# Stick-breaking attention with two heads in a step, and LRU input parts queued behind the gates

## The chip, the cores and the metric

The kernel runs on one core of a Trainium2 chip. The metric is the device time of one execution in microseconds (us). TensorE (PE) multiplies matrices into PSUM, VectorE (DVE), ScalarE (ACT) and GpSimd (POOL) work elementwise, SyncE (SP) only issues DMAs here. Each engine takes its instructions strictly in the order of its own list and waits on semaphores for the others; PEld rows are TensorE's weight loads.

## The reference, cut to what matters

Two blocks are computed for 1024 positions of width 1024: a first block of two layers (window attention and memory attention, then an LRU mixer and memory attention, each with an MLP) and a second block with stick-breaking attention (8 heads) and sliding-window attention (8 heads). The change touches the LRU mixer and the stick-breaking attention:

```
# stick breaking, per head: q, k, v of 64 columns
z = q @ k.T * 0.125
log_1mb = where(causal, log_sigmoid(-z), 0.0)
later = reverse cumsum over keys of log_1mb, without the own term
w = where(causal, exp(log_sigmoid(z) + later), 0.0)
y = w @ v

# LRU, per direction (forward and reverse), per block of 128 channels
r = sigmoid(x @ wa + ba); i = sigmoid(x @ wx + bx)
log_a = -8 * r * softplus(-lam); a = exp(log_a)
u = sqrt(-expm1(2 * log_a)) * (i * x)
h[t] = a[t] * h[t-1] + u[t]
```

x of the LRU is a 4-tap convolution of a projection; the sum of both directions is multiplied by the gelu of a second projection.

## The kernel before, in words

Activations are kept transposed (channels on partitions, positions along the row). Every large product is written as three f32r matmuls of high and low parts (`project`). Weights arrive in blocks of 128x1024: `load` brings a block into one of NR buffers `raw` (4 before), `split` makes its high part on ACT and its low part on DVE (on POOL for the LRU layer's blocks) into `wsp`, two blocks ahead of TensorE, and a buffer of `raw` is loaded again as soon as its block is split. The program writes every engine's list by hand, in the order of the Python code; `Queues.add` adds an instruction with its waits.

**LRU.** For each of 8 channel blocks n: `lru_g(n)` evacuates the gelu projection, `lru_x(n+1)` the input projection of the next block and its convolution (one ACT instruction, then three DVE `STT`), `gates(n)` has four groups of six matmuls (`xs`, the split input parts, times `lruw`) with a Tanh each, then per direction Tanh, Exp, Square on ACT and the `v` product on DVE, then the gelu's Tanh, two Sqrt, the products `u` and the two scans (L1040). POOL adds the directions (L1042) and `L["late"]` multiplies by the gelu on DVE. `lru_parts(n+1)` makes the high part of the next block's input on ACT and the low part on DVE; before, it is called behind `gates(n)`, so its two instructions stand behind the square roots and the scans.

**Stick breaking.** A step is one head (par) of a pair (pr), a half of the queries (hf, 512 columns) and a key block kb of 128, from the last key block to the first; there are 96. On the diagonal a step covers only 128, 256 or 384 columns, so that of the 12 key blocks of a pair 6 are of full width and 2 each of 384, 256 and 128. A step does: scores z on TensorE; on DVE min(z/8, 40) from PSUM; on ACT Exp and Ln(1+.), which is softplus; on DVE max with z/8 (`STT`), on POOL its high part (CAST, L1253), on DVE its low part; on TensorE two matmuls with a triangle (`triI`) that add the sum within the block onto z in PSUM, and two with all ones (`onesN`) that add the block's whole sum to a running bank `AB` of the head; ACT copies z out of PSUM into `tw`, DVE adds the running bank, ACT takes Exp, and TensorE multiplies with v, whose columns are padded with 64 zeros so that both heads add into one bank. The parts of a step lie up to five steps apart on the engines' lists, with four score banks and three buffers of each kind.

Of the kernel before, what the change touches and what calls it, by code (L numbers as in the profile page):

```python
# [113 lines left out]
def program(nc, D, out, stop=None, dbg=None):  # L114
    ctx = ExitStack()
    with ctx:
# [34 lines left out]
        NR, NS, LA = 4, 3, 2  # L151
# [538 lines left out]
        def window_units(Qt, Kt, Vt, pairs, tiles, nbs, outf, bias, sinkv):  # L690
            units = []
            for n in range(8):
                for kp in range(pairs):
                    kbs = [n + d for d in nbs if 0 <= n + d < 8]
                    for half in range(2):
# [13 lines left out]
                        def pv(pts, ob, fr, n=n, kp=kp, kbs=kbs, half=half):  # L709
                            for j, (pt, c) in enumerate(pts):  # L710
                                for par in range(2):
                                    st = Vt[:, kbs[j], kp, 128 * par:128 * par + 64]
# [99 lines left out]
        Vt = place(48 * KB, [128, 8, 2, 192])  # L812
        MQ = place(64 * KB, [128, 4, 1024])
        pool(lambda e: e.memset(Vt[:, :, :, 64:128], 0.0), *kv_done)
# [37 lines left out]
        def rows_to(Tv, by_rms, *after):  # L852

            def ev(views, op):
                ends = []
                for t, v in enumerate(views):
                    C = v.shape[1] // 128
                    src = v.rearrange("p (c a d) -> p c a d", c=C, a=2)
                    dst = Tv[:, t, :, :].rearrange("p c (a d) -> p c a d", a=3)[:, :, 0:3:2, :]
# [142 lines left out]
        def gates(n):  # L1002

            gp = []
            for gi in range(4):
# [9 lines left out]
                if gi % 2 == 0:  # L1015
                    a = A(trs[d], ps, ACT.Tanh, op, L.get(("v", d)), L["r"], lam_ready, scale=0.5, bias=V("ba", i1))
                    L["tr"] = a
# [11 lines left out]
            L[("xc", n)] = [L[("o1", 1)], L["xs"], L["xsh"]]  # L1029
            a = A(gq, gq, ACT.Tanh, L["gq"], scale=0.7978845608028654)  # L1030
# [17 lines left out]
        for n in range(8):  # L1048
# [6 lines left out]
            if n < 7:  # L1055
                lru_parts(n + 1)
# [94 lines left out]
        SV = place(64 * KB, [128, 8, 4, 192])  # L1151
# [3 lines left out]
        pool(lambda e: e.memset(SV[:, :, :, 64:128], 0.0), *sv_free)  # L1155
# [21 lines left out]
        me = [place(o_ * KB, [128, 512]) for o_ in (28, 30, 94)]  # L1177
        sps = place(16 * KB, [128, 3, 2, 512], F32R)
        tw = place(88 * KB, [128, 3, 512])
        triI, onesN = triR[:, 0, :], triR[:, 1, :]  # L1180
        ZB, AB, OBK = (0, 1, 2, 3), (4, 5), (6, 7)
        steps = []
        grp = 0
        for pr in range(4):
            for hf in range(2):
                top = 4 * hf + 3
                for kb in range(top, -1, -1):
                    for par in range(2):
                        steps.append((pr, hf, kb, par, top, grp))
                grp += 1  # L1190
        n_s = len(steps)
        F = [dict() for _ in range(n_s)]
        got = lambda s, key: F[s].get(key) if s >= 0 else None

        def view(s):
            pr, hf, kb, par, top, grp = steps[s]
            c0 = max(0, kb - 4 * hf) * 128
            return (c0, PS[:, ZB[s % 4], c0:512], me[s % 3][:, c0:512], sps[:, s % 3, 0, c0:512],
                    sps[:, s % 3, 1, c0:512], tw[:, s % 3, c0:512], PS[:, AB[par], c0:512])

        def pe_scores(s):
            pr, hf, kb, par, top, grp = steps[s]
            c0, z = view(s)[:2]
            rows = slice(64 * par, 64 * par + 64)
            if kb == top and par == 0:
                ob = OBK[grp % 2]
                mm(PS[:, ob, :], zerob, cb[:, 0:512], True, False, c_cb, free[ob], skip_group_check=True)
            o = mm(z, SK[rows, pr, kb * 128:(kb + 1) * 128], SQ[rows, pr, 512 * hf + c0:512 * hf + 512], True, False,
                   free[ZB[s % 4]], skip_group_check=True)
            if kb >= 4 * hf:  # L1210
                o = mm(z[:, 0:128], identb, maskD, False, False, c_cb, skip_group_check=True)
            F[s]["qk"] = o

        def pe_cum(s):
            c0, z, m, sh, sl, t, ab = view(s)
            pr, hf, kb, par, top, grp = steps[s]
            if kb == top:
                F[s]["zero"] = mm(PS[:, AB[par], :], zerob, cb[:, 0:512], True, False, c_cb, free[AB[par]],
                                  skip_group_check=True)
            mm(z, triI, sh, False, False, F[s]["sh"], skip_group_check=True)  # L1220
            F[s]["cum"] = mm(z, triI, sl, False, True, F[s]["sl"], skip_group_check=True)

        def pe_carry(s):
            c0, z, m, sh, sl, t, ab = view(s)
            if steps[s][2] > 0:
                mm(ab, onesN, sh, False, False, F[s]["add"], skip_group_check=True)
                F[s]["carry"] = mm(ab, onesN, sl, False, False, skip_group_check=True)
            else:
                free[AB[steps[s][3]]] = [F[s]["add"]]
                F[s]["carry"] = None  # L1230

        def pe_values(s):
            pr, hf, kb, par, top, grp = steps[s]
            c0, z, m, sh, sl, t, ab = view(s)
            ob = OBK[grp % 2]
            o = mm(PS[:, ob, c0:512], SV[:, kb, pr, 64 * par:64 * par + 128], t, False, False, F[s]["w"],
                   skip_group_check=True)
            F[s]["pv"] = o
            if kb == 0 and par == 1:
# [3 lines left out]
        for s in range(n_s + 6):  # L1243
            v = s - 5
            if 0 <= v < n_s:
                pe_values(v)
            if s < n_s:
                pe_scores(s)
            v = s - 2
            if 0 <= v < n_s:  # L1250
                c0, z, m, sh, sl, t, ab = view(v)
                o = STT(m, z, 0.125, m, ALU.mult, ALU.max, F[v]["ln"])
                F[v]["sh"] = pool(lambda e, sh=sh, m=m: e.tensor_copy(sh, m), o, got(v - 3, "carry"),  # L1253
                                  got(v - 3, "cum"))
            v = s - 3
            if 0 <= v < n_s:
                c0, z, m, sh, sl, t, ab = view(v)
                F[v]["sl"] = TT(sl, m, fz(sh), ALU.subtract, F[v]["sh"], got(v - 3, "carry"), got(v - 3, "cum"))
                pe_cum(v)
            v = s - 4  # L1260
            if 0 <= v < n_s:
                c0, z, m, sh, sl, t, ab = view(v)
                F[v]["add"] = TT(t, t, ab, ALU.add, F[v]["zc"], got(v - 2, "carry"), F[v].get("zero"))
                pe_carry(v)
            if s < n_s:
                c0, z, m, sh, sl, t, ab = view(s)
                F[s]["min"] = TS(m, z, 0.125, 40.0, ALU.mult, ALU.min, F[s]["qk"], got(s - 3, "sl"), got(s - 3, "sh"))
            v = s - 1
            if 0 <= v < n_s:
                c0, z, m, sh, sl, t, ab = view(v)  # L1270
# [213 lines left out]
```

How the kernel before makes its waits and increments, by code:

```python
            def run(eng):  # L93
                seen = {}
                for o in self.q[name]:
                    for d in o.deps:
                        if seen.get(d.sem.name, 0) < d.val:
                            eng.wait_ge(d.sem, d.val)
                            seen[d.sem.name] = d.val
                    if o.fn is None:
                        continue
                    ins = o.fn(eng)
                    if o.sem is not None:
                        ins.then_inc(o.sem, 1 if o.sem is self.sems.get(name) else 16)
```

## Time and profile before

| | us |
|---|---|
| median of 2 runs | 3499.54 (3499.21 to 3499.87) |
| the profiled execution | 3512.42 |
| its span in the trace | 3510.6 |
| PE busy | 3225.2 (92%) |
| DVE busy | 1690.7 (48%) |
| ACT busy | 1084.7 (31%) |
| POOL busy | 392.4 (11%) |

The span is from the first to the last recorded instruction; the profiled execution's own time is 1.8 us more. Busy shares are averages over stages that have different limits, so a stage is read by itself: the LRU loop lies at 1474 to 1740 us of the span, stick breaking at 2913 to 3163 us.

### The profile page before, as it was taken

The page shows a single profiled execution, that of the slowest core. Times are in us where ns is not written, and L with a number is a line of the kernel's source. Part 1 is how long each engine was busy: PE and PEld are TensorE (multiplying, and loading weights), DVE is VectorE, ACT ScalarE, POOL GpSimd, SP SyncE. Part 2 cuts the span into 40 slices and gives each one's busy share as a digit, 9 for nine tenths or more (in the row PEclk, how much of TensorE's full clock was granted, in tenths as well). Part 3 has the DMA queues.
Part 4 walks back from the last instruction along what each step waited for, and adds up shares of the span by engine and source line. Part 5 has one row for each costly group of instructions (what it writes and reads, how often), then busy time and mean ns, then how long its engine had stood idle before and what let it go on. Part 6 is the DMA issues. An engine that isn't in the chain of part 4 may idle for free.

```text
span 3510.6 us, 35191 instructions
## 1 busy us (share of the span) xinstructions
PE 3225.2 (92%) x14288; PEld 2467.7 (70%) x14298; DVE 1690.7 (48%) x2178; ACT 1084.7 (31%) x1845; POOL 392.4 (11%) x313
## 2 busy tenths in 40 slices
PE   4999988999999999989879999999997999999768
PEld 4776546778888888767648788888885775548546
DVE  6544863254444433688642433333335416881355
ACT  4202652121111111466541211111114316771332
POOL 0001531000000000244310000000003102230120
PEclk9999999999999999999999999999998998999899
DMA  4210002122222211211211111111111310001012
GB/s 165 84 36 31 1 1 77 43 67 72 72 72 72 72 45 54 66 42 33 66 60 42 42 48 48 48 48 44 47 48 54 114 48 7 1 1 54 19 65 91
DMA packets 52578, 184.96 MB, mean 53 GB/s; under 512 B 5825, under 2 KB 6209, under 8 KB 52289
## 3 DMA queue, kind: packets, MB, share of 16 engines
q1 hardware_dynamic: 52416, 182.71, 16.0%
q8 instruction: 113, 1.85, 0.2%
q14 instruction: 49, 0.39, 0.0%
HBM read 169.06 MB, written 13.63 MB: 52 GB/s over the span
## 4 chain that ended last, share of the span: by engine, by line
PE 76%; DVE 10%; ACT 8%; issue 3%; POOL 3%; DMA 0%; SPq 0%; DVEq 0%; POOLq 0%; ACTq 0%
PE PS L281 75%; ACT p L138 6%; DVE p L141 3%; DVE p L144 2%; DVE sm L463 2%; PE PS L498 2%; POOL p L489 2%; DVE p L1040 1%; ACT H L138 1%; POOL p L1042 1%; ACT L138 1%; ACT wsp L138 1%; DVE p L511 0%; DVE wsp L141 0%; DVE p L379 0%
## 5 line engine op out<-in xcount | busy, mean ns | idle before, releaser
L281 PE MATMUL PS<-H,wsp 128*128 128x512 f32 x6864 | 1601.9, 395 | 65.0 <-ACT p L138 21.5
L281 PEld LDWEIGHTS PS<-H,wsp 128*128 128x128 f32 x6864 | 1302.6, 190 | 359.0 <-ACT p L138 38.2
L281 PE MATMUL PS<-p,wsp 128*128 128x512 f32 (+1 forms) x3840 | 904.4, 396 | 54.5 <-DVE p L141 23.7
L281 PEld LDWEIGHTS PS<-p,wsp 128*128 128x128 f32 x3840 | 720.3, 192 | 233.3 <-ACT wsp L138 37.8
L138 ACT ACTIVATE p<-p 128x512 f32<-128x512 f32 (+5 forms) x522 | 354.9, 690 | 1008.6 <-DVE p L144 679.9
L138 ACT ACTIVATE wsp<-raw 128x1024 fp32r<-128x1024 f32 (+1 forms) x262 | 271.5, 1038 | 856.7 <-PE PS L281 681.2
L141 DVE TENSOR_TENSOR p<-p,PS 128x1024 f32<-128x1024 f32 (+3 forms) x248 | 229.5, 926 | 501.9 <-PE PS L281 497.3
L141 DVE TENSOR_TENSOR wsp<-raw,wsp 128x1024 fp32r<-128x1024 f32 x234 | 287.8, 1233 | 268.7 <-ACT wsp L138 268.7
L281 PE MATMUL PS<-p 128*64 128x256 f32 (+8 forms) x1432 | 377.9, 478 | 16.3 <-DVE p L144 5.5
L141 DVE TENSOR_TENSOR p<-PS,p 128x1024 f32<-128x1024 f32 (+1 forms) x124 | 142.6, 1155 | 455.9 <-PE PS L281 428.8
L141 DVE TENSOR_TENSOR p<-p 128x1024 fp32r<-128x1024 f32 (+8 forms) x267 | 219.6, 824 | 105.5 <-ACT p L138 103.8
L281 PEld LDWEIGHTS PS<-p 64*128 64x128 f32 (+2 forms) x1432 | 166.2, 182 | 120.8 <-ACT p L138 61.0
L138 ACT ACTIVATE p<-PS 128x512 f32<-128x512 f32 (+4 forms) x245 | 136.8, 573 | 283.0 <-PE PS L281 253.9
L489 POOL TENSOR_SCALAR p<-p,sm 128x256 f32<-128x256 f32 (+2 forms) x128 | 149.4, 1172 | 617.9 <-DVE sm L482 617.9
L498 PE MATMUL PS<-cf,p 128*128 128x128 f32 x600 | 95.5, 297 | 101.6 <-POOL p L489 89.8
L144 DVE SCALAR_TENSOR_TENSOR p<-p 128x1024 f32<-128x1024 f32 (+1 forms) x119 | 165.6, 1406 | 34.4 <-POOL p L1042 18.4
L138 ACT ACTIVATE p<-PS,sm 128x256 f32<-128x256 f32 (+2 forms) x256 | 127.7, 508 | 173.7 <-DVE sm L144 123.6
L231 POOL TENSOR_TENSOR wsp<-raw,wsp 128x1024 fp32r<-128x1024 f32 (+1 forms) x28 | 66.7, 2383 | 925.0 <-ACT wsp L138 925.0
L498 PEld LDWEIGHTS PS<-cf,p 128*128 128x128 f32 x600 | 69.6, 150 | 141.4 <-issue 89.5
L463 DVE TENSOR_REDUCE sm<-PS 128x2 f32<-128x768 f32 (+3 forms) x96 | 94.9, 988 | 54.8 <-PE PS L281 54.4
L379 POOL TENSOR_TENSOR p<-p 128x512 f32<-128x512 f32 x14 | 20.6, 1470 | 862.7 <-DVE p L379 832.5
L1253 POOL CAST p<-p 128x512 fp32r<-128x512 f32 (+3 forms) x96 | 69.9, 729 | 292.8 <-DVE p L144 153.5
(74 smaller groups left out, 1527.9 us busy)
## 6 DMA issues: line engine op xcount, KB each, us to landing
raw<-in_dn_dram SPq DMA_DIRECT2D x68, 512.0 KB, 3.5
raw<-in_in_dram SPq DMA_DIRECT2D x66, 512.0 KB, 3.5
raw<-in_up_dram SPq DMA_DIRECT2D x64, 512.0 KB, 3.5
raw<-in_out_dram SPq DMA_DIRECT2D x40, 512.0 KB, 3.5
p<-in_ada_dram SPq DMA_DIRECT2D x24, 512.0 KB, 4.4
raw<-in_kv_dram SPq DMA_DIRECT2D x16, 512.0 KB, 4.2
p<-in_x_dram SPq DMA_DIRECT2D x16, 512.0 KB, 9.7
spill_dram<-p SPq DMA_DIRECT2D x16, 512.0 KB, 2.9
```

The costliest lines, as they stand in the source:

```text
L138: return act(lambda e: e.activation(o, i, f, **kw), *a)
L141: return dve(lambda e: e.tensor_tensor(o, x, y, op), *a)
L144: return dve(lambda e: e.scalar_tensor_tensor(out=o, in0=x, scalar=s, in1=y, op0=op0, op1=op1), *a)
L231: o2 = pool(lambda e: e.tensor_tensor(l, src, fz(h), ALU.subtract), o1, uses.get(b - NS), loads[b], splits.get(b - NS))
L281: return pe(lambda e: e.matmul(o, l, r, start=start, stop=stop, **kw), *a)
L379: lambda e: e.tensor_tensor(self.acc, self.acc, sq, ALU.add), a, self.op)
L463: o = dve(lambda e: e.tensor_reduce(mx, S, AX.X, ALU.max), op, prev)
L489: last[1] = pool(lambda e, P_=P_, r=r: e.tensor_scalar(P_, P_, r, None, ALU.mult), o)
L498: o = pe(lambda e, t_out=t_out, t_in=t_in: e.transpose(t_out, t_in, ident), probs[J * u + j], free[b])
L1040: L[("h", d)] = dve(lambda e, dst=dst, da=da, du=du: e.tensor_tensor_scan(out=dst, data0=da, data1=du, initial=0.0, op0=ALU.mult, op1=ALU. ...
L1042: o = pool(lambda e: e.tensor_tensor(Y[:, n, :], Y[:, n, :], tis[1], ALU.add), L[("h", 0)], L[("h", 1)])
L1253: F[v]["sh"] = pool(lambda e, sh=sh, m=m: e.tensor_copy(sh, m), o, got(v - 3, "carry"), got(v - 3, "cum"))
```

## The change

1. LRU: `lru_parts(n + 1)` is called inside `gates(n)`, right behind the four gate groups; the Tanh, Exp, Square of both directions are moved from inside the groups to behind it.
2. Stick breaking: a step holds both heads of a pair (48 steps). Two score matmuls go to rows 0 to 63 and 64 to 127 of the array and to two banks. ACT copies both banks to SBUF first (`t`), and min and max read that copy. The within-block sums and the carried sums go into one bank per head (`PB`), where the carry now uses a strict triangle `triS` in place of all ones, so that within plus carry make the block's whole sum. The low part is made on POOL in three steps of four, on DVE in the fourth (v % 4 == 3). A pair of value matmuls writes partitions 0 to 63 and 64 to 127. At most three steps are in the lists at once; there are two score pairs, three `t`, two `m`, two `sps`.
3. The padding of v goes in all three attentions with its POOL memsets; the copies that fill v write whole rows. `raw` has 3 buffers in place of 4.

```
-        NR, NS, LA = 4, 3, 2
+        NR, NS, LA = 3, 3, 2
...
                     L[("o1", d)] = STT(tis[d], tis[d], 1.0, xcs[n % 2], ALU.add, ALU.mult, a, L["made"])
-                    a3 = A(Tts[d], trs[d], ACT.Tanh, L["tr"], L.get(("u", d)), scale=c4[:, i1:i1 + 1],
-                           bias=c4[:, i1:i1 + 1])
-                    a4 = A(ats[d], trs[d], ACT.Exp, a3, L.get("h"), scale=nc4[:, i1:i1 + 1], bias=nc4[:, i1:i1 + 1])
-                    a5 = A(trs[d], ats[d], ACT.Square, a4)
-                    L[("a", d)] = a4
-                    L[("v", d)] = STT(Tts[d], trs[d], 1.0, Tts[d], ALU.add, ALU.mult, a5)
                 free[2 * p] = free[2 * p + 1] = [a]
             L["gates"] = op
             L[("xc", n)] = [L[("o1", 1)], L["xs"], L["xsh"]]
+            if n < 7:
+                lru_parts(n + 1)
+            for d in range(2):
...
+                a5 = A(trs[d], ats[d], ACT.Square, a4)
...
             gates(n)
-            if n < 7:
-                lru_parts(n + 1)
             L["late"]()
...
+        for s in range(n_s + 3):
+            if 0 <= s - 3:
+                pe_carry(s - 3)
+                pe_values(s - 3)
             if s < n_s:
                 pe_scores(s)
+            if 0 <= s - 2 < n_s:
+                pe_within(s - 2)
+            v = s - 1
+            if 0 <= v < n_s:
+                c0, z, t, m, sh, sl, pb = view(v)
+                o = A(m, m, ACT.Exp, F[v]["min"])
+                o = A(m, m, ACT.Ln, o, bias=1.0)
+                o = F[v]["m"] = STT(m, t, 0.125, m, ALU.mult, ALU.max, o)
+                F[v]["sh"] = pool(lambda e, sh=sh, m=m: e.tensor_copy(sh, m), o, got(v - 2, "carry"))
+                if v % 4 == 3:
+                    F[v]["sl"] = TT(sl, m, fz(sh), ALU.subtract, F[v]["sh"], got(v - 2, "carry"))
+                else:
+                    F[v]["sl"] = pool(lambda e, sl=sl, m=m, sh=sh: e.tensor_tensor(sl, m, fz(sh), ALU.subtract),
+                                      F[v]["sh"], got(v - 2, "carry"))
+            if s < n_s:
+                c0, z, t, m, sh, sl, pb = view(s)
+                F[s]["zc"] = A(t, z, ACT.Copy, F[s]["qk"], got(s - 3, "pv"))
+                free[ZB[s % 2]] = free[ZB[s % 2] + 1] = [F[s]["zc"]]
+                F[s]["min"] = TS(m, t, 0.125, 40.0, ALU.mult, ALU.min, F[s]["zc"], got(s - 2, "sl"), got(s - 2, "sh"))
             v = s - 2
             if 0 <= v < n_s:
+                c0, z, t, m, sh, sl, pb = view(v)
+                F[v]["add"] = TT(t, t, pb, ALU.add, F[v]["cum"], F[v]["m"])
                 F[v]["w"] = A(t, t, ACT.Exp, F[v]["add"], scale=0.125)
```

The lists of the engines, at three places. First ScalarE in one round of the LRU loop, from the table load ahead of the gates (vec: Tanh of a gate group out of PSUM; sm: Tanh and Exp; without either: Square, gelu Tanh, Sqrt, Copy). Before:

```order
L138 ACT_TABLE_LOAD
L138 ACTIVATE p<-PS,vec 128x1024 x2
L138 ACTIVATE p<-p,sm 128x1024 x2
L138 ACTIVATE p<-p 128x1024
L138 ACTIVATE p<-PS,vec 128x1024 x2
L138 ACTIVATE p<-p,sm 128x1024 x2
L138 ACTIVATE p<-p 128x1024 x2
L138 ACT_TABLE_LOAD
L138 ACTIVATE p<-p 128x1024 x3
```

And now:

```order
L138 ACTIVATE p<-PS,vec 128x1024 x4
L138 ACTIVATE p<-p 128x1024
L138 ACTIVATE p<-p,sm 128x1024 x2
L138 ACTIVATE p<-p 128x1024
L138 ACTIVATE p<-p,sm 128x1024 x2
L138 ACTIVATE p<-p 128x1024 x2
L138 ACT_TABLE_LOAD
L138 ACTIVATE p<-p 128x1024 x2
```

The single instruction behind the four gate Tanhs is the copy of `lru_parts`; it was the third behind the second table load.

Second VectorE in the stick-breaking stage (TENSOR_SCALAR: min; SCALAR_TENSOR_TENSOR: max; TENSOR_TENSOR p<-p: low part; TENSOR_TENSOR p<-p,PS: add). Before, two head steps:

```order
L149 TENSOR_SCALAR p<-PS 128x512
L144 SCALAR_TENSOR_TENSOR p<-PS,p 128x384
L141 TENSOR_TENSOR p<-p 128x384
L141 TENSOR_TENSOR p<-p,PS 128x256
L149 TENSOR_SCALAR p<-PS 128x512
L144 SCALAR_TENSOR_TENSOR p<-PS,p 128x512
L141 TENSOR_TENSOR p<-p 128x384
L141 TENSOR_TENSOR p<-p,PS 128x384
```

And now, the second step of these with its low part on VectorE:

```order
L144 SCALAR_TENSOR_TENSOR p<-p 128x1024
L149 TENSOR_SCALAR p<-p 128x1024
L141 TENSOR_TENSOR p<-p,PS 128x1024
L144 SCALAR_TENSOR_TENSOR p<-p 128x1024
L141 TENSOR_TENSOR p<-p 128x1024
L149 TENSOR_SCALAR p<-p 128x2x128
L141 TENSOR_TENSOR p<-p,PS 128x1024
```

Max now comes first, the low part (where VectorE has it) between max and min, and max and min read SBUF alone.

Third TensorE there (64x512: values of one head; 128x512 of p: scores of one head; triR: sums). Before:

```order
L281 MATMUL PS<-p,triR 128x384 x2
L281 MATMUL PS<-p 128x384
L281 MATMUL PS<-p 128x512
L281 MATMUL PS<-p,triR 128x512 x4
L281 MATMUL PS<-p 128x512 x2
```

And now:

```order
L281 MATMUL PS<-p,triR 128x384 x8
L281 MATMUL PS<-p 64x384 x2
L281 MATMUL PS<-p 128x512 x2
L281 MATMUL PS<-p,triR 128x512 x8
L281 MATMUL PS<-p 64x512 x2
```

The eight triR matmuls are four of the step's within-block sum and, behind the wait for VectorE's add of the same step, four of its carry, both ahead of its values.

## Rows read from the trace of the kernel before

**Rows 1.** The page: busy time of each engine.
```profile
PE 3225.2 (92%) x14288; PEld 2467.7 (70%) x14298; DVE 1690.7 (48%) x2178; ACT 1084.7 (31%) x1845; POOL 392.4 (11%) x313
```
**Rows 2.** Windows: stretch, length, busy of PE, PEld, DVE, ACT, POOL, granted clock, DMA.
```profile
2912.00:2973.70 61.70, 59.99 (x184) 30.81 (x187) 42.72 (x90) 41.79 (x88) 15.51 (x22) 0.83 0.00 1
2973.70:3033.50 59.80, 59.32 (x206) 29.57 (x207) 48.26 (x99) 46.55 (x97) 17.54 (x24) 1.00 0.00 1
```
**Rows 3.** Timeline, full-width head step: start, length, engine, instructions, idle before.
```profile
3077.13 1.20 PE L281 MATMUL PS<-p,triR 128*128 128x512 f32 x4
...
3078.16 2.07 PE L281 MATMUL PS<-p 128*128 128x512 f32 x4
...
3078.59 1.01 POOL L1253 CAST p<-p 128x512 fp32r<-128x512 f32 x1 [1.71 <-DVE p L144]
...
3080.16 0.50 PE L281 MATMUL PS<-p,triR 128*128 128x512 f32 x1
```
**Rows 4.** Timeline, window attention: head pairs on both halves of the array.
```profile
317.68 0.70 PE L281 MATMUL PS<-p 64*128 64x256 f32 x4 [1.55 <-DVE p L141]
...
318.31 0.28 PE L281 MATMUL PS<-cb 128*128 128x128 bf16 x2
```
**Rows 5.** Groups of instructions: xcount, busy us, mean ns, idle before.
```profile
L138 ACT ACTIVATE p<-PS 128x1024 f32<-128x1024 f32 x11 | 11.3, 1026 | 96.4 <-PE PS L281 96.4
L138 ACT ACTIVATE p<-p 128x512 f32<-128x512 f32 x24 | 15.1, 627 | 0.8
```
**Rows 6.** Lines' instructions: duration min/median/max in ns.
```profile
L1052 POOL TENSOR_SCALAR p<-p x8: 1050/1900/1905, 1469.3 to 1707.2; 128x1024 f32<-128x1024 f32 x8
L1053 POOL TENSOR_TENSOR p<-p x8: 2339/3229/3254, 1470.5 to 1708.3; 128x1024 f32<-128x1024 f32 x8
```
**Rows 7.** Timeline: a wide min without PSUM; VectorE and GpSimd at once.
```profile
54.60 0.69 DVE L149 TENSOR_SCALAR p<-p 128x1024 f32<-128x1024 f32 x1
...
1542.11 3.25 POOL L1053 TENSOR_TENSOR p<-p 128x1024 f32<-128x1024 f32 x1
1543.13 3.32 DVE L144 SCALAR_TENSOR_TENSOR p<-p,vec 128x1024 f32<-128x1024 f32 x1
...
3343.23 1.08 POOL L489 TENSOR_SCALAR p<-p,sm 128x256 f32<-128x256 f32 x1 [4.86 <-DVE sm L482]
```
**Rows 8.** Timeline of one LRU round.
```profile
1545.51 1.06 ACT L138 ACTIVATE p<-p 128x1024 f32<-128x1024 f32 x1
...
1546.56 7.91 DVE L144 SCALAR_TENSOR_TENSOR p<-p 128x1024 f32<-128x1024 f32 x5
...
1554.34 2.96 ACT L138 ACTIVATE p<-p 128x1024 f32<-128x1024 f32 x3
1555.43 1.23 DVE L141 TENSOR_TENSOR p<-p 128x1024 f32<-128x1024 f32 x1 [0.96 <-ACT p L138]
...
1562.57 3.19 POOL L1042 TENSOR_TENSOR p<-p 128x1024 f32<-128x1024 f32 x1 [13.86 <-DVE p L1040]
1565.71 1.26 POOL L231 TENSOR_TENSOR wsp<-raw,wsp 128x512 fp32r<-128x512 f32 x1
1565.79 2.27 DVE L144 SCALAR_TENSOR_TENSOR p<-p 128x1024 f32<-128x1024 f32 x1 [2.25 <-POOL p L1042]
...
1567.08 5.85 PE L281 MATMUL PS<-p,wsp 128*128 128x512 f32 x24 [2.84 <-issue]
```
**Rows 9.** The chain that ended last: start, length, where it ran, in two rounds.
```profile
1540.95 3.25 ACT p L138 x3
...
1575.17 3.25 ACT p L138 x3
```
**Rows 10.** Windows around and behind a TensorE pause of 3.50 us, and in window attention.
```profile
1575.00:1580.00 5.00, 3.58 (x9) 2.87 (x10) 4.93 (x3) 4.92 (x6) 4.92 (x3) 0.55 0.33 105
3327.00:3334.00 7.00, 3.85 (x31) 2.48 (x32) 4.46 (x9) 3.57 (x11) 1.98 (x2) 1.00 0.00 0
```
**Rows 11.** DMA issues: KB each, us from issue to landing.
```profile
raw<-in_in_dram SPq DMA_DIRECT2D x66, 512.0 KB, 3.5
```

More of the change, by code:

```diff
@@ L1176, in program @@
         ln_exp()
[L1177 to L1190, printed above, removed]
+        t_bufs = [place(o_ * KB, [128, 2, 512]) for o_ in (24, 28, 96)]
+        m_bufs = [place(o_ * KB, [128, 2, 512]) for o_ in (16, 20)]
+        sps = place(80 * KB, [128, 2, 2, 2, 512], F32R)
+        triI, triS = triR[:, 0, :], triR[:, 1, :]
+        ZB, PB, OBK = (0, 2), 4, (6, 7)
+        steps = [(pr, hf, kb) for pr in range(4) for hf in range(2) for kb in range(4 * hf + 3, -1, -1)]
         n_s = len(steps)
@@ L1201, in pe_scores @@
         def pe_scores(s):
-            pr, hf, kb, par, top, grp = steps[s]
+            pr, hf, kb = steps[s]
             c0, z = view(s)[:2]
-            rows = slice(64 * par, 64 * par + 64)
-            if kb == top and par == 0:
-                ob = OBK[grp % 2]
-                mm(PS[:, ob, :], zerob, cb[:, 0:512], True, False, c_cb, free[ob], skip_group_check=True)
-            o = mm(z, SK[rows, pr, kb * 128:(kb + 1) * 128], SQ[rows, pr, 512 * hf + c0:512 * hf + 512], True, False,
-                   free[ZB[s % 4]], skip_group_check=True)
@@ L1223, in pe_carry @@
[L1223 to L1237, printed above, removed]
+            for par in range(2):
+                rows = slice(64 * par, 64 * par + 64)
+                o = mm(z[:, par, :], SK[rows, pr, kb * 128:(kb + 1) * 128],
+                       SQ[rows, pr, 512 * hf + c0:512 * hf + 512], True, False, free[ZB[s % 2]], free[ZB[s % 2] + 1],
+                       skip_group_check=True)
@@ new lines, in pe_scores, with pe_within @@
+            if kb >= 4 * hf:
+                for par in range(2):
+                    o = mm(z[:, par, 0:128], identb, maskD, False, False, c_cb, skip_group_check=True)
+            F[s]["qk"] = o
+        def pe_within(s):
+            pr, hf, kb = steps[s]
+            c0, z, t, m, sh, sl, pb = view(s)
+            if kb == 4 * hf + 3:
+                for par in range(2):
+                    mm(PS[:, PB + par, :], zerob, cb[:, 0:512], True, False, c_cb, p_open[par], skip_group_check=True)
+            for part, op in ((sh, F[s]["sh"]), (sl, F[s]["sl"])):
+                for par in range(2):
+                    o = mm(pb[:, par, :], triI, part[:, par, :], False, False, op, skip_group_check=True)
+            F[s]["cum"] = o
@@ new lines, in pe_carry, with pe_values @@
+        def pe_carry(s):
+            c0, z, t, m, sh, sl, pb = view(s)
+            if steps[s][2] > 0:
+                for part in (sh, sl):
+                    for par in range(2):
+                        o = mm(pb[:, par, :], triS, part[:, par, :], False, False, F[s]["add"], skip_group_check=True)
+                F[s]["carry"] = o
+            else:
+                p_open[:] = [F[s]["add"], F[s]["add"]]
+                F[s]["carry"] = F[s]["cum"]
+        def pe_values(s):
+            pr, hf, kb = steps[s]
+            c0, z, t, m, sh, sl, pb = view(s)
+            ob = OBK[(2 * pr + hf) % 2]
+            if kb == 4 * hf + 3:
+                mm(PS[:, ob, :], zerob, cb[:, 0:512], True, False, c_cb, free[ob], skip_group_check=True)
+            for par in range(2):
+                o = mm(PS[64 * par:64 * par + 64, ob, c0:512], SV[:, kb, pr, 64 * par:64 * par + 64], t[:, par, :],
+                       False, False, F[s]["w"], skip_group_check=True)
```

84 lines of the change are left out of this document (23 added, 61 removed).

## The prediction

> **What bounds the kernel now.** I read the page first: TensorE is busy for 92% of the span [rows 1], but that is a mean over stages, so I asked for the windows of the two stages that change.
>
> Stick breaking: three of the four pairs of heads take 59.80 us each, with TensorE busy for 59.3 and VectorE for 48 (one of them in [rows 2]); the first takes 61.70 at a granted clock of 0.83. The timeline of a full-width head step says why: its four sum matmuls start at 3077.13, the next step's at 3080.16, a period of 3.03 us, in which TensorE streams four f32r matmuls and four passes of fp32 ones (values and scores, two passes each) without a pause that counts [rows 3]. So the stage is bound by TensorE, at 6.1 us for two heads. The four passes of 512 columns take 2.07 us with the tail, about 0.43 us each; an f32r matmul takes about 0.21.
>
> LRU: the chain of waits shows the same pattern from 1540.95 to 1575.17, 34.2 us, and it runs through ScalarE, VectorE and GpSimd, not through TensorE [rows 9]. A round is: gate Tanhs; Square and the rest without a pause; Sqrt at 1554.34; the first product u at 1555.43, whose wait is for ScalarE; scans; GpSimd's sum at 1562.57; the late product at 1565.79, which waits for it; then the evacuations, the convolution's first instruction, a table load and the next Tanh. TensorE starts the gates' matmuls at 1567.08, when the weights' low part is made (GpSimd, 1565.71 for 1.26, behind the sum), not when the input parts are [rows 8].
>
> **The LRU move.** Nothing is added to the round; the copy of the input's high part goes ahead of the two Tanh, Exp, Square chains, the gelu's Tanh and the Sqrts. It was free: its place was the third of the 2.96 us behind the table load, where ScalarE then idles. Now it is in the chain: 1.06 us [rows 8]. It also waits for the convolution. That ended at about 1546.45: the third of its STTs started at 1543.13 and took 3.32 us, blocked by GpSimd's product of 1542.11 [rows 7]. Four Tanhs from 1540.95 at 1.06 end at 1545.2, so ScalarE waits 1.25 us in addition. Sum: 2.3 to 2.5 us a round, seven rounds: +17 us. VectorE's low part moves from behind the scans, where it then waits 2.25 us for GpSimd [rows 8], to before the v products: neither gains nor loses. What was queued behind the moved copy on ScalarE (square roots, the next splits) and on VectorE (u, scans) all shifts with it. The earlier parts let TensorE start nothing earlier, as its gates wait for the weights' low part. Bounds: 0 if the convolution's end and the copy fit in slack that I do not see, 3.5 a round (25 us) if GpSimd blocks one more product.
>
> **The stick-breaking step.** First TensorE. Scores and values of a pair now stand side by side on halves of the array. In window attention four such passes (two heads, two passes each, 256 columns) start at 317.68 and the next matmul at 318.31: 0.63 us, which is three times 0.21 and not two [rows 4]: a matmul's second pass runs beside the next head's first, the outer two alone. At 512 columns a pair is 3 x 0.43 = 1.28 us where two single ones are 1.71. The rule in the Trainium skill, page TensorEngine Tiling (Array Packing), sections Theoretical Speedup and Key Properties, is that tiles run independently with up to twice the rate; by it the pair is 0.85, the stage about 37 us shorter than my sum, and the kernel near 3571. I take the row.
>
> TensorE's work for two heads falls from 6.1 to 2 x 1.28 + 8 x 0.21 + switches 0.3 = 4.6 us. But nothing is now queued deep enough to use it. ScalarE's list is Exp, Ln of step s-1, copy of s, Exp of weights s-2; VectorE's is max s-1, (low part s-1), min s, add s-2. Exp s-1 follows weights s-3, max needs Ln, add stands behind max and min, weights need the add. That is one closed ring. Durations for 1024 elements: ScalarE 1.05 (1.026 from PSUM), VectorE with two inputs 1.22, min from SBUF 0.69, GpSimd's CAST 1.05 (taken from its one-input operation alone; that form has no row of this width), its subtraction 2.35 [rows 5 to 8]. For 512 elements ScalarE takes 0.63 [rows 5]; narrower ones of the others I scale alike.
>
> A plain full step, from the end of the weights of s-3 (0): values 0.05 to 1.35, scores to 2.7, seen by ScalarE at 2.85, copy to 3.9. Beside it Exp and Ln to 2.05, max to 3.3. Then GpSimd starts CAST at 3.35, before min has its input. Operations that read SBUF alone exclude one another on VectorE and GpSimd: the STT of 1.2 us above took 3.32, and a one-input product of only 256 elements took GpSimd 1.08 us beside two of VectorE [rows 7], where 1024 elements alone take 1.05 [rows 6]. So min waits until 4.4, ends 5.1; add to 6.25; weights to 7.3. **7.3 us against 6.1.** Without the exclusion it is 6.8.
>
> A step with its low part on VectorE: max to 3.3, CAST to 4.4, low part to 5.6, min 6.3, add of the narrower or equal step, weights to 8.1. The fourth step is always of full width (v = 3, 7, 11 of 12), so three of twelve rounds carry it.
>
> The twelve rounds of a pair of heads, each added up so with its own widths (the scores' s, max's s-1, add's s-2, values' s-3): 8.2, 5.7, 4.9, 7.3, 7.7, 5.4, 4.9, 7.3, 8.1, 7.3, 7.3, 7.3, sum 81.4 us against 59.8. The fourth and eighth (scores 512, max 384) rest on GpSimd's subtraction starting just ahead of min; otherwise each is 5.6. Four pairs: +86; start and drain of the pipeline cost 250 - 239 = 11 us before with six steps in flight and some 5 with three double ones: -6. **Stage +80 us.** From below, the ring alone without TensorE or exclusion is 6.2 for a plain step, about 73 for a pair, stage +45; from above, every step blocked by a GpSimd subtraction, +110.
>
> **The clock.** TensorE pauses 2.4 us in a plain step (sums done at 3.6, carry after the add) and 4.4 us in one with VectorE's low part. Behind a pause of 3.50 us in the LRU loop the granted clock was 0.55 for 5 us, so mostly the lower level, 1.2 GHz; in window attention, busy 3.85 of 7.00, it stays at 1.00 [rows 10]. I take a drop behind each of the twelve long pauses for one step, and at 1.2 GHz a plain step is 2.4 us longer (values and scores 5.1, then min behind GpSimd's subtraction), half of it on the path: +12 us, between 0 and 35.
>
> **At nothing.** Padding gone: memsets are covered by GpSimd's idle time, and the copies of v have the same elements. Three raw buffers: a block lands 3.5 us after issue [rows 11] and is split three blocks later, over 7 us on even in the shortest (kv) blocks; without that cover up to 3 us at the start.
>
> **Sum.** 80 + 17 + 12 = 109 us. The profiled execution is 3512.42, 0.4% above the median of 3499.54; durations are the same, so I add to the median: **3608 us** (3.1% more).
>
> **Rivals.**
> - *The pairs run at twice the rate or VectorE wins the races, and the LRU copy costs half:* stage +45, LRU +9, clock 0: 3554. For: two races are within 0.1 us; against: the 0.63 us row and two in-order lists. 0.20.
> - *The ring hides and TensorE stays the bound* (faster): if Exp of s-1 overlapped the add of s-2 enough, a step would cost 4.6/6.1 of before, 59.8 x 0.25 x 4 = -59, and earlier parts would save the 2.84 us pause ahead of the gates, seven times: -20. 3420. It decides if a full round is under 6.1 us. Against: ScalarE and VectorE each wait for the other once a round by their lists. 0.05.
> - *The clock stays low for the whole stage:* 24 full steps +2.4, 24 narrow ones +0.8, together 77 in place of 12: 3673. For: the first pair had 0.83 even with TensorE busy [rows 2]. 0.12.
> - The forecast has the rest, 0.63, own range 3575 to 3640.
>
> The range of 8 in 10 is 3550 to 3658: to the first rival's time and well towards the third's. A measurement of this kernel tells about 2%, 70 us, from no change, so the line is 3569.5. Faster 0.03 (most of the second rival), same 0.22 (the first, a little of the forecast), slower 0.75.
>
> **What would show it.** After: a pair of heads at 78 to 85 us; plain full steps 7.3 us apart; min 1.0 to 1.1 us late behind a CAST; idle of TensorE ended by ScalarE's weights and, on VectorE, low parts waiting for CAST; LRU rounds of 36.5 to 36.8 us with a pause of ScalarE behind the fourth Tanh; clock under 0.95 in the stage. A full step under 6.8, rounds of 34.2 or a pair under 70 would make it wrong.

## The result, and the profile after

The change makes the kernel slower: 3626.68 us, the median of two executions (3614.14 and 3639.23) against 3499.54, a ratio of 1.036 (95% interval 1.021 to 1.052). Run again in four executions it took 3612.57 (3611.94 to 3644.08), ratio 1.033 (1.029 to 1.038). The forecast was 3608. The profiled execution of the changed kernel took 3614.14, that of before 3512.42: the two traces are 101.7 us apart, and that is what I account for here.

Windows of the changed kernel (stretch, length, busy time of PE, PEld, DVE, ACT, POOL, granted clock, DMA) over the whole stick-breaking stage, its third pair of heads, and pieces of 4 us in it:

```profile
2915.86:3263.87 348.01, 227.56 (x824) 104.04 (x825) 153.51 (x164) 156.31 (x193) 103.06 (x84) 0.81 0.00 0
3038.86:3124.16 85.30, 55.76 (x206) 25.78 (x206) 38.22 (x41) 38.77 (x49) 25.78 (x22) 0.82 0.00 0
3046.00:3050.00 4.00, 3.36 (x10) 1.74 (x12) 1.06 (x2) 2.85 (x3) 0.00 (x0) 0.50 0.00 0
...
3062.00:3066.00 4.00, 0.38 (x3) 0.33 (x3) 3.58 (x2) 0.39 (x1) 1.90 (x1) 1.00 0.00 0
3066.00:3070.00 4.00, 4.00 (x12) 1.15 (x10) 1.23 (x1) 2.67 (x3) 0.00 (x0) 0.57 0.00 0
...
3094.00:3098.00 4.00, 3.00 (x21) 1.71 (x21) 1.55 (x3) 2.44 (x5) 1.97 (x2) 1.00 0.00 0
```

And the kernel before over its whole stage:

```profile
2912.89:3163.04 250.15, 245.88 (x816) 122.61 (x824) 193.28 (x392) 186.47 (x385) 69.95 (x96) 0.96 0.00 1
```

Both stretches run from the first score matmul to the first of the next projection. The stage grew by 97.9 us. [Rows 2] had 59.80 us for a pair of heads with TensorE busy for 59.3; now it is 85.30, and no engine is busy for more than 56. In the full-width steps much of TensorE's work is done at a low clock (0.50 and 0.57 in two of the pieces), and the 1.00 of 3062 to 3066 goes to a piece in which it has 0.38 us of work. It is not so in the whole pair: among the narrow steps, 3094 to 3098, TensorE works 3.00 of 4 us at 1.00.

The timeline of the changed kernel around one full-width step (start, length, engine, instructions, idle before it), in place of [rows 3]:

```profile
3049.53 1.23 DVE L144 SCALAR_TENSOR_TENSOR p<-p 128x1024 f32<-128x1024 f32 x1 [2.94 <-ACT p L138]
3050.82 1.04 POOL L1256 CAST p<-p 128x1024 fp32r<-128x1024 f32 x1 [6.96 <-DVE p L144]
...
3051.82 1.02 ACT L138 ACTIVATE p<-PS 128x1024 f32<-128x1024 f32 x1 [2.33 <-PE PS L281]
3051.94 2.36 POOL L1260 TENSOR_TENSOR p<-p 128x1024 fp32r<-128x1024 f32 x1
3052.88 1.97 DVE L149 TENSOR_SCALAR p<-p 128x1024 f32<-128x1024 f32 x1 [2.13 <-ACT p L138]
3054.77 1.21 DVE L141 TENSOR_TENSOR p<-p,PS 128x1024 f32<-128x1024 f32 x1
...
3056.03 1.93 PE L281 MATMUL PS<-p,triR 128*128 128x512 f32 x4 [2.63 <-DVE p L141]
```

Max ends at 3050.8, GpSimd's CAST runs, the copy out of PSUM ends only at 3052.8 because the scores came slowly, and by then GpSimd is in its subtraction of 2.36 us. Min, 0.69 us long where nothing is in its way [rows 7], takes 1.97 and ends 0.55 us behind that subtraction (3054.85 against 3054.30), as if it had begun only when GpSimd was through; the add and TensorE's carry stand behind it. This circle (values and scores, copy, min, add, the weights' Exp, the next values) is what I call the ring.

The LRU round of the changed kernel. In [rows 8] the copy stood behind the square roots, and GpSimd's sum took 3.19:

```profile
1507.83 4.13 ACT L138 ACTIVATE p<-PS,vec 128x1024 f32<-128x1024 f32 x4
1513.36 1.06 ACT L138 ACTIVATE p<-p 128x1024 fp32r<-128x1024 f32 x1 [1.39 <-DVE p L144]
...
1517.73 1.21 DVE L141 TENSOR_TENSOR p<-p 128x1024 fp32r<-128x1024 f32 x1
...
1531.93 2.34 POOL L1043 TENSOR_TENSOR p<-p 128x1024 f32<-128x1024 f32 x1 [16.34 <-DVE p L1041]
```

From the first round's gate Tanhs to the last one's there are seven rounds: 236.18 us before (1473.20 to 1709.38), 247.65 now (1472.44 to 1720.09), so 33.74 and 35.38 a round, +11.5. The 101.7 us are: -0.8 up to the LRU, +11.5 to the projection behind it (1735.86, now 1746.58), -7.8 in the 1177 us from there to the stage, where the change touches only the weights' buffers and the layout of v, +97.9 in the stage, +0.9 behind it. The -7.8 is of the size by which executions differ outside the two stages: the kernel with the steps alone (below) comes to the stage 17.9 us before the changed one, of which the LRU rounds are 11.5, and the kernel of before with only its values matmuls changed (below) comes there 11.4 us before this execution of the kernel before.

### The profile page after: what moved, and what is told of

It is laid out like the page before. It is cut to its first block, busy times and chain, and to the rows that moved or that the text cites. A ratio compares the mean times of both kernels' runs of the same rounds, so it can differ in the third digit from the quotient of the medians.

```text
span 3612.4 us, 34695 instructions
## 1 busy us (share of the span) xinstructions
PE 3197.3 (89%) x14298; PEld 2443.2 (68%) x14298; DVE 1651.4 (46%) x1950; ACT 1055.5 (29%) x1653; POOL 416.4 (12%) x298
## 4 chain that ended last, share of the span: by engine, by line
PE 72%; DVE 13%; ACT 8%; issue 4%; POOL 3%; DMA 0%; SPq 0%; DVEq 0%; POOLq 0%; ACTq 0%
PE PS L281 70%; ACT p L138 7%; DVE p L141 4%; DVE p L144 3%; DVE sm L463 2%; PE PS L498 2%; POOL p L489 1%; DVE p L1041 1%; ACT H L138 1%; DVE p L149 1%; DVE p L511 0%; POOL p L1043 0%; DVE wsp L141 0%; ACT wsp L138 0%; ACT L138 0%
## 5 line engine op out<-in xcount | busy, mean ns | idle before, releaser
L138 ACT ACTIVATE p<-p 128x1024 f32<-128x1024 f32 (+4 forms) x378 | 323.4, 875 | 1110.1 <-DVE p L144 688.5
L141 DVE TENSOR_TENSOR p<-p,PS 128x1024 f32<-128x1024 f32 (+2 forms) x200 | 222.2, 1111 | 499.6 <-PE PS L281 499.6
L281 PE MATMUL PS<-p 128*64 128x256 f32 (+9 forms) x1432 | 324.4, 525 | 32.1 <-ACT p L138 22.6
L144 DVE SCALAR_TENSOR_TENSOR p<-p 128x1024 f32<-128x1024 f32 (+3 forms) x167 | 211.9, 1277 | 148.4 <-ACT p L138 124.9
L141 DVE TENSOR_TENSOR p<-p 128x1024 fp32r<-128x1024 f32 (+5 forms) x183 | 181.7, 995 | 119.1 <-ACT p L138 103.8
L281 PEld LDWEIGHTS PS<-p 128*64 128x64 f32 (+2 forms) x1432 | 132.9, 184 | 145.7 <-issue 86.1
L138 ACT ACTIVATE p<-PS 128x512 f32<-128x512 f32 (+3 forms) x197 | 129.0, 674 | 315.5 <-PE PS L281 286.8
L281 PE MATMUL PS<-p,triR 128*128 128x512 f32 (+3 forms) x352 | 106.4, 433 | 100.4 <-DVE p L141 100.1
L281 PEld LDWEIGHTS PS<-p,triR 128*128 128x128 f32 x352 | 68.2, 230 | 141.4 <-DVE p L141 112.7
```

The source lines that it names most:

```text
L138: return act(lambda e: e.activation(o, i, f, **kw), *a)
L141: return dve(lambda e: e.tensor_tensor(o, x, y, op), *a)
L144: return dve(lambda e: e.scalar_tensor_tensor(out=o, in0=x, scalar=s, in1=y, op0=op0, op1=op1), *a)
L281: return pe(lambda e: e.matmul(o, l, r, start=start, stop=stop, **kw), *a)
```

## The experiments

**The LRU move alone**, on the kernel before:

```
             L[("xc", n)] = [L[("o1", 1)], L["xs"], L["xsh"]]
+            if n < 7:
+                lru_parts(n + 1)
+            for d in range(2):
...
             gates(n)
-            if n < 7:
-                lru_parts(n + 1)
```

The loop over d holds the Tanh, Exp, Square and `v` that stood inside the gate groups.

> The kernel before with the LRU part of the change alone. My theory: the chain of a round gets the copy of the input's high part (1.06 us) and ScalarE's wait for the convolution (1.39 us in the changed kernel), and loses the time that GpSimd's sum of the directions was held back by VectorE's low part (3.19 us before, 2.34 after), so 1.6 us a round, seven rounds: 3499.5 + 11 = 3511, rounds of 35.5 us. Rival (my prediction's own sizing): 2.4 us a round and no gain at the sum: 3516.5. Other rival, earlier parts help: at or below 3499.5.

3509.44 us against 3501.73, ratio 1.0022 (1.0010 to 1.0035), +8 us (3.5 to 12). Rounds are 35.4 us, and GpSimd's sum takes 2.34; the chain of waits of this kernel has the last step of the convolution, 3.32 us long, ahead of the copy:

```profile
1503.12 3.32 DVE p L144
1506.46 2.21 ACT p L138 x2
```

**The steps alone**: the changed kernel with the LRU order of before.

> The changed kernel with the LRU loop of the kernel before. Theory: all but 11 us of the change is the stick-breaking stage, +91 us in the profiled execution, so 3590 to 3595 in executions like the profiled one and up to 3620 in others, as TensorE's clock there differs from execution to execution. Rival: the two parts influence each other through the clock, or three raw buffers and v without padding cost something: over 3620, or pre-stage times that differ from before by over 2 us.

3605.06 us, ratio 1.0289 (1.0269 to 1.0310), the stage 348.07 us at a clock of 0.81, as in the changed kernel. The stage does not depend on the LRU part, and the steps carry nine tenths. The four executions (3601.28 to 3611.52) lie above the 3590 to 3595 that I expected for one like the profiled one, and below the 3620 that I allowed for others. The rival's sign, a difference of over 2 us ahead of the stage, came by the letter and says nothing: this execution reaches the stage 15.0 us earlier than the profiled one of the kernel before, and the kernel with only its values changed, whose list ahead of the stage is that of before, reaches it 11.4 us earlier.

**The changed kernel again**, as it is:

> The changed kernel as it is, once more: its two executions so far lay 25 us apart (3614 and 3639, mean clock 0.954 and 0.942). Theory (the stage takes 348 us in each, the two parts add 98 and 12 us, and the rest is the clock of single executions elsewhere): median 3605 to 3620, ratio 1.030 to 1.035, above the kernel with the steps alone (3605) by the LRU's 8 to 12. Rival (the change lowers the clock outside its stages too): median 3625 or more, ratio over 1.035.

3612.57, so 8 us over the steps alone, as expected. The execution that was profiled here took 3644.08, and its trace says where such a one loses. Its stage:

```profile
2917.93:3286.12 368.19, 248.99 (x817) 114.98 (x825) 159.23 (x164) 156.33 (x193) 100.49 (x84) 0.73 0.00 0
```

20.2 of the 29.9 us more than 3614.14 lie in this stage, at a clock of 0.73 in place of 0.81: the same list of instructions took 348 us at the one clock and 368 at the other.

**Zeros in TensorE's pauses.** Eight bf16 matmuls of zeros per step, added to a bank that is being summed, so that TensorE does not pause.

```
+                if steps[s - 2][2] != 4 * steps[s - 2][1] + 3:
+                    for _ in range(8): mm(PS[:, OBK[...], :], zerob, cb[:, 0:512], False, False, c_cb)
```

> The changed kernel with eight bf16 matmuls by a matrix of zeros behind the within-block sums of each step but a half's first, into the open bank of values (adds zero). They fill TensorE's pause of 2.4 us with 1.7 us of work. Theory that the lower clock costs 85.3 - 81.4 us a pair and more in other executions: the clock of the stage rises from 0.82 to over 0.95, a pair of heads takes 79 to 83 us, plain full steps all near 7.3 us in place of 9.6, total 3590 to 3602, and the executions differ by under 5 us. Rival: the clock is not on the path (the steps are 9.6 us for another reason): pairs stay at 85 us or get longer by TensorE's added work, 3614 or more.

3586.46, ratio 1.0233; the stage 322.9 us at 0.91, 25.1 less. (These expectations count the stage from a mark 6.9 us behind the first scores: 341, 316 and 326.5 there are 348.0, 322.9 and 333.4 here.) The clock is on the path, though work was added. The theory's sizes missed: the clock stayed under 0.95, the total fell below 3590, and the executions still differed by 11 us. In three pairs the last two plain full steps took 6.25 us, in place of the 7.3 that I expected; in the last pair all three were still 9.2 to 9.6.

**GpSimd's CAST behind the next min.** On GpSimd the CAST and the subtraction of a step wait until the next step's min is through.

```
-                F[v]["sh"] = pool(... tensor_copy(sh, m), o, got(v - 2, "carry"))
+                # behind min(s), where v % 4 != 3:
+                F[v]["sh"] = pool(... tensor_copy(sh, m), F[v]["m"], got(v - 2, "carry"), F[s]["min"])
```

> The changed kernel with GpSimd's CAST and subtraction of a step waiting for VectorE's next min (where the low part is GpSimd's); nothing else moves. Theory that min is held up by GpSimd's lock on SBUF (min 1.97 to 2.46 us in place of 0.69 in the changed kernel): min takes 0.69, a full plain step loses 1.3 to 1.8 us (9.6 to about 8 at the lower clock, 7.3 to 6.9 at the full), some 8 steps of 12 gain, a pair takes 74 to 80 us, total 3614 - 20 to 3614 - 45, 3570 to 3595. Rival: min only looks long and waits for something else, or the later low part puts the within-block sums behind the add: no change or longer, 3614 to 3640.

3597.57, ratio 1.0267; the stage 333.4 us, 14.6 less at an even lower clock (0.78). The wide min in the changed kernel and here (xcount, busy us, mean ns, idle before):

```profile
L149 DVE TENSOR_SCALAR p<-p 128x1024 f32<-128x1024 f32 x24 | 37.0, 1541 | 28.2 <-ACT p L138 28.2
```

```profile
L149 DVE TENSOR_SCALAR p<-p 128x1024 f32<-128x1024 f32 x24 | 16.6, 693 | 21.5 <-ACT p L138 21.2
```

In the changed kernel 12 of these 24 mins took 1.97 to 2.46 us and the others 0.69 to 1.12; here all take 0.69, so 20.4 us of waiting are gone, 0.85 a min on average. Work on GpSimd is later and the stage shorter, by less than the theory had: the first three pairs took 80 to 86 us where it gave 74 to 80, and the total lies just above its 3595.

**No low part on VectorE** (`if v % 4 == 3` becomes `if False`):

> The changed kernel with one edit: no step has its low part on VectorE, GpSimd makes all of them. In the changed kernel three of a pair's twelve steps carry it there (8.79, 7.97 and 8.45 us long), with VectorE waiting for GpSimd's CAST ahead of it. Theory (GpSimd's work blocks min): the 1.22 us and the wait go, but in those steps too min now meets GpSimd's subtraction, and at the lower clock it loses: the two narrow ones (8.79, 7.97) gain 1 to 2 us, the wide one goes to 9.4: stage 348 to 340 to 350, total 3605 to 3617. Rival (VectorE's own work is what the step waits for): each of the three at 6.2 to 6.8, stage 325 to 330, total 3595. Rival (no change at all, since GpSimd is then the late one): stage 348.

3601.61, ratio 1.0276; the stage 334.8 us, 13.2 less, min still 1.50 us. That is below the theory's 340 and above the rival's 330, so neither is right alone, and how much each has is not shown. The plain full steps were 8.7 to 10.5 us long with mins of up to 2.7 us, all but one, which took 6.25 with a min of 0.69.

**Zeros and CAST:**

> The changed kernel with both edits: eight zero matmuls a step in TensorE's pause, and GpSimd's CAST held until the next step's min is through. Singly the stage went from 341 us to 316 (zeros) and to 326.5 (CAST). Theory (one ring, two things lengthen it, the clock and a min that is kept waiting by GpSimd, and they feed each other): min at 0.69 us everywhere, full steps at 6.2 us in every pair of heads, so the sum of the two gains less what both had already: stage 300 to 308, total 3570 to 3585. Rival (they are the same 25 us: the zeros gained only by letting min through): stage 314 to 318, total 3583 to 3592. Rival (the ring without blocking and at full clock is TensorE-bound or better than the kernel before): stage under 260.

3565.63, ratio 1.0192, the stage 309.9 (303.0 from the other mark) at 0.92: in the stage the gains add, 38.1 us where the two singly gave 39.7. The total fell 4 us below the theory's range.

**All three:**

> The changed kernel with three edits: zero matmuls in TensorE's pauses, GpSimd's CAST behind the next min, and no low part on VectorE. With the first two the stage took 309.9 us, a plain full step 6.25, and the steps with VectorE's low part 8.3, 8.0 and 8.7. Theory (what is left is the ring itself, 6.25 us for a full step, and VectorE's low part is on it): those three fall to 6.3, 4.8 to 6.3 and 6.3, 6 us for a pair of heads: stage 284 to 290, total 3540 to 3548, still 35 us behind the kernel before, because a full ring of 6.25 is no shorter than two single steps of 3.03. Rival (GpSimd's 3.4 us of CAST and subtraction, started behind min, come too late for the within-block sums): stage 305 to 315.

3530.12, ratio 1.0080 (1.0058 to 1.0102). The stage is far shorter than I expected:

```profile
2913.77:3178.84 265.07, 241.24 (x1123) 111.83 (x1145) 123.49 (x152) 155.21 (x193) 127.37 (x96) 0.99 0.00 1
```

265.1 us, at a clock of 0.99, which none of the kernels with part of these edits had. Plain full steps are 6.25 us, and a pair of heads 64.9. So 82.9 of the 97.9 us were the clock, the held-up min and VectorE's low part together; 15 are left. The low part on VectorE, worth 13.2 us when it was taken away alone, is worth 44.9 once the other two are gone (309.9 against 265.1), and the clock rises with it from 0.92 to 0.99.

The trace also shows what a plain full step then waits for:

```profile
3030.70 2.14 PE L281 MATMUL PS<-p 128*64 128x512 f32 x8
...
3032.67 1.23 DVE L144 SCALAR_TENSOR_TENSOR p<-p 128x1024 f32<-128x1024 f32 x1 [3.16 <-ACT p L138]
...
3032.88 1.03 ACT L138 ACTIVATE p<-PS 128x1024 f32<-128x1024 f32 x1 [0.24 <-PE PS L281]
...
3033.94 0.69 DVE L149 TENSOR_SCALAR p<-p 128x1024 f32<-128x1024 f32 x1
```

Values and scores, then the copy out of PSUM, end at 3033.91; the other way round, Exp, Ln and max, ends at 3033.90. Min, the add (1.22 us) and the weights' Exp (1.05) stand behind both. The two arms tie, so making only one of them shorter should not shorten the step; that is read from the trace, and no run tests it.

**All three without the zeros:**

> The changed kernel with GpSimd's CAST behind the next min and no low part on VectorE, as in the kernel with all three edits (stage 265.1 us, granted clock 0.99, min 0.69), but without the zero matmuls. It tells what the lower clock costs once nothing blocks VectorE. Theory (the clock falls with TensorE's pauses, and at the lower level values and scores take twice as long with half of it on the path): clock 0.75 to 0.85, stage 285 to 300, total 3550 to 3565. Rival (with the pauses down to 1.5 us the clock stays up without help): clock over 0.95, stage 262 to 268, total 3530 or a little less, since TensorE is spared the zeros. Rival (the lower clock matters only through GpSimd's blocking of min): clock about 0.8, stage under 275.

3573.62, ratio 1.0193, the stage 309.3 us:

```profile
2915.15:3224.42 309.27, 226.08 (x824) 101.87 (x825) 124.08 (x152) 156.02 (x193) 127.12 (x96) 0.79 0.00 0
```

The mins take 0.69, and yet the stage is 44 us longer than with the zeros: the lower clock costs that with no min held up, more than the theory's 20 to 35, and the rival that it matters only through GpSimd falls. Both stage times are of one execution each; the totals differ by 43.5 us between the medians and by 35.4 between the fastest executions. The three causes are not a sum of fixed amounts. Of the zeros' two prices, 25 us with the others in place and 44 without, the second is the clean one: with the others in place the zeros brought the clock only to 0.91.

**Values side by side in the kernel before**, still one head a step:

```
-            o = mm(PS[:, ob, c0:512], SV[:, kb, pr, 64 * par:64 * par + 128], t, ...
+            o = mm(PS[64 * par:64 * par + 64, ob, c0:512], SV[:, kb, pr, 128 * par:128 * par + 64], t, ...
...
-            v = s - 5
-            if 0 <= v < n_s:
-                pe_values(v)
+            if s % 2 == 0 and 0 <= s - 6 < n_s:
+                pe_values(s - 6)
+                pe_values(s - 5)
```

> The kernel before, one head a step, with one edit: the values matmuls of the two heads of a pair are issued side by side (on the two halves of the array's columns) every second step, as the changed kernel has them; everything else as before. Theory (a pair of fp32 matmuls of two passes each takes three passes and not four, the row of 0.63 us in window attention): 0.43 us saved for each two full heads, widths summed 9 full ones for a pair of heads, 3.9 us a pair of heads, stage 250 to 235, total 3484 to 3490. Rival (twice the rate): 0.85 us for each two, stage 219, total 3468. Rival (the switch between array shapes and the longer queue eat it): stage 248 to 252, total 3497 to 3501.

3490.18, ratio 0.9971 (0.9960 to 0.9981): a little faster than the kernel before, clear of the interval though only by 0.3%, with the stage at 239.2 us, 10.9 less. Its timeline has the rate of a pair. At the stage's end both heads' values for one block are four matmuls, and, where a head is alone, two:

```profile
3134.95 1.08 PE L281 MATMUL PS<-p 128*64 128x512 f32 x4
...
3136.81 1.07 PE L281 MATMUL PS<-p 128*64 128x512 f32 x2
```

Four side by side take as long as two, 1.08 and 1.07 us. That is twice the rate, not four thirds. The same kernel has the scores of one head over 256 columns, two passes with nothing beside them, ahead of the same small matmul as in [rows 4]:

```profile
2967.78 0.70 PE L281 MATMUL PS<-p 64*128 64x256 f32 x2 [0.69 <-ACT p L138]
2968.41 0.45 PE L281 MATMUL PS<-cb 128*128 128x128 bf16 x2
```

They take 0.70 us and 0.63 from start to start, exactly what the four of two heads take in [rows 4]. So the 0.63 was two passes of 0.21 and about 0.2 us that a single head pays too, and not three passes. TensorE's busy time in the stage fell by 24.1 us, of which 10.9 came out: a full step of two heads went from 6.06 to 5.66, and TensorE now waits for ScalarE (14.4 us in the stage). The total lay at the upper end of the theory's, its stage of 235 was missed by 4, and the mechanism was the rival's.

**The low part of the LRU input later**, on the kernel before: out of GpSimd's way, into the next round's pause of VectorE.

> The kernel before, with VectorE's subtraction for the low part of the LRU input taken from behind the scans to a place in the next round where VectorE idles 2.07 us, and nothing moved on ScalarE. GpSimd's sum (3.19 us, beside that subtraction) is then alone. Theory (the round's end hangs on that sum and it takes 2.34 us alone, as in the changed kernel): rounds of 33.9 become 33.0 to 33.1, seven times: total -6 us, ratio 0.998. Rival (what the forecast said: the move of the low part neither gains nor loses): rounds 33.9, ratio 1.000. Rival (it gets in the way of the next product): rounds longer, +5 us.

3506.63, ratio 1.0020 (1.0011 to 1.0029), slower. Its chain of waits:

```profile
1565.52 3.50 DVE p L141 x3
...
1569.15 5.15 PE PS L281 x12
```

GpSimd's sum did fall to 2.39, as expected, but now the gates' matmuls wait for the low part, and TensorE, which was not on the round's chain before, stands on it: 34.0 to 34.7 us a round in place of 33.7 on average, 3.9 us over the seven. The idle place in the next round only looked free from VectorE: what stands there comes too late for TensorE.

**Both edits of before:**

> The kernel before with both edits: values side by side in the stick-breaking stage and the LRU input's low part later. They lie in different stages, so the two gains add: if -12 and -6 then -18, total near 3482, ratio 0.995. Rival: neither gains, ratio 1.000.

3502.39, ratio 1.0004 (0.9995 to 1.0013), so the sum that I expected missed by 20 us. The stage kept its gain (239.4 us), and the LRU's seven rounds took 1.4 us more than before (237.62). The two effects measured singly, -10 and +7, would give 3497; where the other 5 us lie is not shown, and the rest of the list differs by as much between executions. The kernel with the values side by side alone stays the fastest.

## Why the prediction was right, and where not

The direction, the total (109 forecast; 101.7 between the traces, 105 between the medians of the repeated run, 127 between the first medians) and the place (stick breaking +92 with the clock, measured +97.9) were right. Several steps under it were not, and that the total came so near is in part luck. Over a pair of heads at the clock granted, the three plain full steps took 6.2 us more than in my sum of 81.4, the fourth and eighth 4.2 us less, and the other seven 1.9 more.

- **"In the chain: 1.06 us" and "ScalarE waits 1.25 us in addition"** were right: 1.06, and a pause of 1.39 ahead of the copy. **"Neither gains nor loses" was wrong**: with VectorE's low part away from behind the scans, GpSimd's sum fell from 3.19 to 2.34. A round therefore costs 1.06 + 1.39 - 0.85 = 1.6 us, measured 1.64, and the LRU 11.5 us and not 17. I had [rows 8] with a sum of 3.19 and [rows 7] with 1.2 us that took 3.32 beside GpSimd, and did not apply the second to the first.
- **"A matmul's second pass runs beside the next head's first, the outer two alone"** was wrong. [Rows 4] give from one start to the next 0.63 us, and I read three passes of 0.21 out of it; the runs show four passes side by side in the time of two (1.08 and 1.07 us). The Trainium skill, page TensorEngine Tiling (Array Packing), section Theoretical Speedup, says that tiles run with up to twice the rate, and the trace agrees with it and not with me. At 512 columns the values and scores of a pair take 2.07 us together from start to start (3030.70 to 3032.77 in the kernel with all three edits), where I had 2 x 1.28 = 2.56. That takes 0.49 off my 6.8 for a plain full step with nothing blocked: 6.3, measured 6.25. The 37 us that I gave for twice the rate do not follow from my rows either: nine full widths a pair of heads, 0.86 us each, are 31 us in four pairs.
- **The clock, +12 us, was too small.** I took a drop behind each of the twelve long pauses, one step each, with pauses of 4.4 us in the steps with VectorE's low part and 2.4 in plain ones. It was the other way round: TensorE paused 2.7 to 3.2 us in the first and up to 3.6 in the plain full steps. The clock was 0.82 over the pairs, and down to 0.50 in single pieces of the full steps. With nothing else in the way it costs 44 us (309.3 against 265.1), and in the changed kernel as it is at least the 25 that the zeros gave back. The range that I gave, 0 to 35, held one of the two.
- **Min behind GpSimd** was the right mechanism with its victim mistaken. I had it lose to the CAST (to 7.3 us a full step); under the lower clock its input comes 1 us later, and it loses to the subtraction, at 9.67, 9.06 and 9.39 us for the three plain full steps at the end of a pair (from one values matmul to the next). The fourth and eighth steps, which I said "rest on GpSimd's subtraction starting just ahead of min", went the other way, 5.25 and 5.17 us in place of 7.3 (I had named 5.6 for that case). Over a pair the twelve are 8.79, 6.21, 4.79, 5.25, 7.97, 5.79, 4.79, 5.17, 8.45, 9.67, 9.06 and 9.39: 85.3 against my 81.4 at full clock.
- **Low parts on VectorE that wait for CAST** were there: 13.6 us of such waits before twelve of them, and their removal gave 13.2 us alone and 44.9 with the other two edits in place. I had priced such a step at 0.8 us over a plain one (8.1 against 7.3).
- **"From below, the ring alone is ... about 73 for a pair"** was a bound only with VectorE's low part in the steps: with it the shortest pair took 75.0 (zeros and CAST), without it 64.9. The 6.2 for a plain full step was right (6.25).
- **At nothing**: the padding and the three `raw` buffers cost nothing that can be told: up to the LRU loop the changed kernel is 0.8 us ahead, and behind the stage it takes 348.5 us where it took 347.6, while the kernels whose list there is that of before take 343.7 to 352.5.
- **The signs that I set**: a pair of heads (85.3 us), rounds of 35.4 in place of 36.5 to 36.8 and plain full steps of over 9 us in place of 7.3 lay outside what I had named; the pause behind the fourth Tanh (1.39), the low parts waiting for CAST and the clock under 0.95 came.

The rivals: the first had two of its conditions come true (the pairs run at twice the rate, and VectorE wins the race in the fourth and eighth steps) and not its time, 3554, since the clock and GpSimd's subtraction took more than that gave. The second, which kept TensorE as the bound, needed a full step under 6.1 us. Even cleared, it is 6.25, 15 us of stage more than before, with TensorE busy for 241 us of which a part is zeros. The third, a low clock for the whole stage, 3673, was not reached, even by the execution with a clock of 0.73 (3644.08). Why one execution gets a clock of 0.81 in the stage and another 0.73 stays open.

## What to carry to other kernels

Making steps twice as wide with half as many in flight took work from the engine that bounded here and handed the time to a ring of dependencies; add up the ring of one wide step against two narrow ones before the busy times. When TensorE began to pause, its lower clock lengthened the ring that made it pause, and what one cause cost depended on whether the others were there (the low part 13 or 45 us, the clock 25 or 44): price them together and not one by one. And an instruction of GpSimd that is ready early can be the costly one: here it was worth 15 us to start it later.

## What the runs showed of the hardware

- fp32 matmuls of two heads on halves of the array: four of 512 columns in 1.08 us, two in 1.07; of 256 columns four and two alike in 0.70.
- A VectorE min of 1024 elements from SBUF took 0.69 us alone and 1.97 to 2.46 us where GpSimd's subtraction (2.35 us) ran; GpSimd's own sum took 3.19 us beside a VectorE subtraction and 2.34 without.
- bf16 matmuls of zeros in TensorE's pauses, with nothing else changed, raised the granted clock of the stage from 0.79 to 0.99 and took 44 us off it.
